# A two-layer hybrid block on one core: all input units of the second mixer in rounded halves

## The reference, cut to what matters

```
p = x @ w_in                               # 1024 x 6144: 24 units of 256 columns
p_rwkv, p_conf, p_short, p_gate = split(p) # 7, 2, 3 and 12 units
y_a = rwkv7(p_rwkv)   # a linear recurrence over time, 8 heads of 64; it normalizes the key kk by head
y_b = silu(layernorm(causal_conv31(u))) @ w_o, u = p_conf[:256] * sigmoid(p_conf[256:])
y_c = (gb * causal_conv3(gc * h)) @ w_o
g = sigmoid(p_gate)
x = layernorm(alpha * x + (g_a*y_a + g_b*y_b + g_c*y_c) @ w_out)
x = layernorm(alpha * x + feed_forward(x)) # dense in layer 0, 8 experts with top 2 in layer 1
```

## Time and profile before

| | |
|---|---|
| median of 3 runs | 2674.24 us (2672.26 to 2674.87) |
| the profiled execution | 2675.59 us, its span 2673.8 us |
| mean granted TensorE clock | 0.981 of full speed |
| TensorE busy | 2580.9 us, 97% of the span |
| VectorE busy | 1787.9 us, 67% |
| ScalarE busy | 1251.7 us, 47% |
| the two mixers | about 889 to 1223 us and 1414 to 1748 us |

### The profile page before, as it was taken

The page is one execution under the profiler, slowest core; times in us unless marked ns, Lnnn a source line. Parts: engine busy times, 40 slices in busy tenths (PEclk is TensorE's granted clock), DMA queues, the critical chain, the costliest instruction groups (busy, mean ns, idle before and its releaser), DMA issues.

```text
span 2673.8 us, 41063 instructions
## 1 busy us (share of the span) xinstructions
PE 2580.9 (97%) x16370; PEld 2186.1 (82%) x16370; DVE 1787.9 (67%) x2178; ACT 1251.7 (47%) x1443; POOL 116.3 (4%) x125
## 2 busy tenths in 40 slices
PE   7999999999999999999998999989999999999997
PEld 6886998878799988767998887678888888888886
DVE  5654776855577546345545553378988988988988
ACT  4442544542344331113334211057777777777775
POOL 1100000200000001200000111000000000000000
PEclk9999999999999999999999999989999999999999
DMA  6333543423455331135553321289999999998995
GB/s 250 111 142 142 184 183 128 152 95 128 181 183 187 141 126 65 64 126 197 189 186 130 110 80 64 79 317 349 351 358 341 349 355 346 346 357 346 347 360 204
DMA packets 77035, 558.16 MB, mean 209 GB/s; under 512 B 8673, under 2 KB 8801, under 8 KB 9569
## 3 DMA queue, kind: packets, MB, share of 16 engines
q1 hardware_dynamic: 76032, 550.93, 55.3%
q0 software_dynamic: 864, 5.24, 0.5%
HBM read 555.09 MB, written 1.05 MB: 208 GB/s over the span
## 4 chain that ended last, share of the span: by engine, by line
PE 60%; issue 35%; DVE 3%; ACT 2%; DMA 1%; POOL 0%; SPq 0%; POOLq 0%; DVEq 0%; ACTq 0%
PE bank L612 25%; PE bank L587 9%; PE bank L635 7%; PE bank L663 4%; PE bank L597 4%; PE bank L621 1%; DMA cst<-in_cst 1%; PE bank L896 1%; PE bank L881 1%; PE bank L893 1%; PE bank L739 1%; PE bank L723 1%; PE bank L731 1%; PE bank L722 1%; DVE ring_lo L1608 1%
## 5 line engine op out<-in xcount | busy, mean ns | idle before, releaser
L2162 DVE TENSOR_TENSOR w_lo<-ring,w_hi 128x2048 fp32r<-128x2048 f32 x216 | 486.3, 2289 | 53.9 <-ACT w_hi L1464 52.8
L1464 ACT ACTIVATE w_hi<-ring 128x2048 fp32r<-128x2048 f32 x216 | 405.1, 1917 | 20.5 <-PE bank L1060 16.9
L1060 PE MATMUL bank<-w_hi,xe_hi 128*128 128x512 f32 x792 | 311.2, 393 | 1.2
L1529 DVE TENSOR_TENSOR w_lo<-ring,w_hi 128x2048 fp32r<-128x2048 f32 x99 | 226.8, 2291 | 125.2 <-ACT w_hi L1159 122.9
L1060 PE MATMUL bank<-w_hi,xe_lo 128*128 128x512 f32 x792 | 308.5, 390 | 0.0
L1060 PE MATMUL bank<-w_lo,xe_hi 128*128 128x512 f32 x792 | 308.5, 390 | 0.0
L612 PE MATMUL bank<-x_hi,w_hi 128*128 128x256 f32 x1056 | 300.1, 284 | 0.8 <-DVE x_lo L1520 0.7
L612 PE MATMUL bank<-x_lo,w_hi 128*128 128x256 f32 x1056 | 299.6, 284 | 0.0
L612 PE MATMUL bank<-x_hi,w_lo 128*128 128x256 f32 x1056 | 299.5, 284 | 0.0
L1159 ACT ACTIVATE w_hi<-ring 128x2048 fp32r<-128x2048 f32 x99 | 189.5, 1914 | 219.3 <-DMA ring<-in_stream 113.8
L587 PE MATMUL bank<-xT,ring 128*128 128x256 f32 x1088 | 256.2, 388 | 1.1 <-ACT Z L1387 1.1
(11 more groups left out here) (340 smaller groups left out, 4868.5 us busy)
## 6 DMA issues: line engine op xcount, KB each, us to landing
ring<-in_stream SPq DMA_DIRECT2D x431, 1024.0 KB, 4.9
yT<-in_stream SPq DMA_DIRECT2D x54, 1024.0 KB, 6.4
xT<-in_stream SPq DMA_DIRECT2D x27, 1024.0 KB, 6.8
Z<-in_stream SPq DMA_DIRECT2D x8, 1024.0 KB, 7.8
norm_rows<-in_rows POOLq DMA_DIRECT2D x4, 1024.0 KB, 7.8
cst<-in_cst SPq DMA_DIRECT2D x1, 1889.0 KB, 20.6
par<-in_par SPq DMA_DIRECT2D x1, 1502.0 KB, 17.2
xres<-in_x SPq DMA_DIRECT2D x2, 512.0 KB, 7.0
```

The lines of the kernel that those rows point to most:

```text
L1060: r = mm(banks[4 + j % 2], a[:, k, :], moe_part(b, i)[:, q * 512:(q + 1) * 512], start=(k == 0 and a is xe_hi and b is w_hi), stop=(k == K ...
L1464: act_(moe_part(w_hi, at), moe_slot(at), ACT.Copy).then_inc(*A.done("moe_hi", at))
L1529: v.tensor_tensor(part(w_lo, n), slot(f0 + n), part(w_hi, n).bitcast(F32), ALU.subtract)\
L2162: v.tensor_tensor(moe_part(w_lo, at), moe_slot(at), moe_part(w_hi, at).bitcast(F32), ALU.subtract)\
```

## The change

Units 7 to 23 of the mixer are also multiplied as rounded halves: three fp32r matmuls for each product in place of one float32 product. Each of these 17 units gets a copy by ScalarE and a subtraction by VectorE. The high halves rotate over five buffers (`LATE_HI`) that lie in memory which is free at the time; `late_user(n)` is the unit that used the buffer before, and the copy waits until TensorE has finished it. ScalarE does the copy of unit n + 2 just before it evicts unit n, or just after where the buffer was unit n's own. The subtractions are put by hand into VectorE's list (`split(7)` to `split(23)`).

The float32 copies of the transposed x (`xT_out`) go; the halves of x move to `x1_hi` and `x2_lo`, the latter in the place of `norm_rows`. So GpSimd loads `norm_rows` for the first layer norm only when the last input unit is done, no longer at the kernel's start and after layer 0.

The fill of the start stage is 6, 18, 4 in place of 12, 12, 4: `kksum` comes six quarters earlier. Taps are spread otherwise: 4 ahead of the gram, 2 and then one at each step in the levels of p = 0, then 2, 2 and 4 in the two chunks of p = 0, 4 in level 0 of p = 1 and 2 in level 1. `short_conv` moves from the levels of p = 0 to the last level of p = 1. Some scratch buffers of the levels move in memory.

```diff
+        x2_lo = rounded("x2_lo", 0, KT * SEQ, norm_rows_at).rearrange("p (k n) -> p k n", k=KT)
         mix_hi = rounded("mix_hi", 6144, SPLIT * UNIT)
+        late_hi = [[rounded(f"late_hi{n}", at, UNIT, gates_at)] for n, at in enumerate((0, UNIT, 2 * UNIT))]
+        late_hi += [[rounded("late_hi3", 15872, UNIT)],
+                    [rounded("late_hi4", 15872 + UNIT, UNIT // 2), rounded("late_hi5", 0, UNIT // 2, yT_at)]]
...
-        START_FILL, GRAM_FILL, CHUNK_FILL = (12, 12, 4), 4, (1, 1, 1)
+        LATE_HI = {n: i for i, ns in enumerate(((9, 12), (8, 11, 14, 16), (7, 10, 13, 15, 17), (18, 20, 22), (19, 21, 23))) for n in ns}
...
+        def late_user(n):
...
+            return max((m for m in LATE_HI if m < n and LATE_HI[m] == LATE_HI.get(n)), default=None)
+
+        START_FILL, GRAM_FILL, CHUNK_FILL = (6, 18, 4), 4, (1, 1, 1)
...
+                    sp.wait_ge(*(T.of("sumsq", l, len(QK_PAIRS) - 1) if u < MIX2_0 else T.of("unit", (MIX2_0, MIX2_1)[l] + N_IN2 - 1)))
+                    if u >= MIX2_0:
+                        sp.wait_ge(*T.of("o", l, 3))
                 sp.dma_start(slot(u), stream[u]).then_inc(s_slot[HOME[u]], 16)
...
                 def quarter(n, q):
-                    u = u0 + n
+                    u, c = u0 + n, q // 2
                     if q == 0:
-                        pe.wait_ge(*loaded(u))
+                        pe.wait_ge(*V.of("lo", u))
                         pe.wait_ge(*(V.of("shift", l, n - 4) if n - 4 < 7 else A.of("in2", l, n - 4)))
-                    r = features(banks[4 + n % 4], slot(u), q // 2, range(4 * (q % 2), 4 * (q % 2) + 4))
+                    for k in range(4 * (q % 2), 4 * (q % 2) + 4):
+                        at = k * 256 + c * P
+                        hi = late_hi[LATE_HI[n]]
+                        whole = hi[0][:, at:at + P] if len(hi) == 1 else hi[k // 4][:, at % 1024:at % 1024 + P]
+                        for w, x in ((whole, x1_hi), (whole, x2_lo), (slot_lo(u)[:, at:at + P], x1_hi)):
+                            r = mm(banks[4 + n % 4][:, c * SEQ:(c + 1) * SEQ], w, x[:, k, :],
+                                   start=(k == 0 and w is whole and x is x1_hi), stop=(k == KT - 1 and w is not whole))
                     if q == 3:
                         r.then_inc(*T.done("unit", u))
                 for n in range(7):
                     pe.wait_ge(*V.of("lo", u0 + n))
-                    if n == 2:
-                        pe.wait_ge(*A.of("xT", "b2", l))
-                        pe.wait_ge(*V.of("xT", "b2", l))
                     if n >= 4:
                         pe.wait_ge(*V.of("shift", l, n - 4))
-                    features_split(banks[4 + n % 4], (part(mix_hi, n), slot_lo(u0 + n)), (x_hi, x_lo),
+                    features_split(banks[4 + n % 4], (part(mix_hi, n), slot_lo(u0 + n)), (x1_hi, x2_lo),
...
 
+                    if n >= N_IN2:
+                        return
                     sc.wait_ge(*loaded(u0 + n))
-                    if n >= SPLIT:
-                        sc.wait_ge(*T.of("unit", u0 + n - SPLIT))
-                    act_(part(mix_hi, n), slot(u0 + n), ACT.Copy).then_inc(*A.done("hi", u0 + n))
+                    if n < 7:
+                        if n >= SPLIT:
+                            sc.wait_ge(*T.of("unit", u0 + n - SPLIT))
+                        act_(part(mix_hi, n), slot(u0 + n), ACT.Copy).then_inc(*A.done("hi", u0 + n))
+                        return
+                    if late_user(n):
+                        sc.wait_ge(*T.of("unit", u0 + late_user(n)))
+                    if n == 18:
+                        sc.wait_ge(*V.of("ends", l))
+                    parts = late_hi[LATE_HI[n]]
+                    for i, to in enumerate(parts):
+                        w = UNIT // len(parts)
+                        act_(to, slot(u0 + n)[:, i * w:(i + 1) * w], ACT.Copy).then_inc(*A.done("hi", u0 + n))
                 if l == 0:
...
                     split(n)
-                x_hi_out("b2", l, None)
-                sc.wait_ge(*V.of("x_lo", "b2", l, KT - 1))
-                xT_out("b2", l, None)
+                x_hi_out("b2", l, None, x1_hi)
...
                 sc.wait_ge(*V.of("omu", l))
                 for n in range(7):
-                    if n + 2 < 7:
+                    split(n + 2)
+                    unit(n)
+
+                def unit_and_split(n):
+                    if late_user(n + 2) != n:
                         split(n + 2)
                     unit(n)
-                fill = Filler(lambda n, q: None, unit)
+                    if late_user(n + 2) == n:
+                        split(n + 2)
+                fill = Filler(lambda n, q: None, unit_and_split)
...
+                    parts = [part(mix_hi, n)] if n < 7 else late_hi[LATE_HI[n]]
+                    for i, hi in enumerate(parts):
+                        at = slice(i * (UNIT // len(parts)), (i + 1) * (UNIT // len(parts)))
+                        v.tensor_tensor(slot_lo(u)[:, at], slot(u)[:, at], hi.bitcast(F32), ALU.subtract).then_inc(*V.done("lo", u))
...
-                x_lo_out("b2", l, None)
-                xT_out("b2", l, None)
+                x_lo_out("b2", l, None, x1_hi, x2_lo)
...
+                split(7)
                 ve.wait_ge(*A.of("sig", l))
...
                         .then_inc(*V.done("cum", l))
+                split(8)
+                split(9)
                 for i in range(2):
                     ve.wait_ge(*T.of("kksum", l, 1))
                     v.tensor_scalar(flat(t3)[:, i * 512:(i + 1) * 512], banks[i], 1e-24, None, ALU.max)\
                         .then_inc(*V.done("kkms", l))
+                split(10)
                 ve.wait_ge(*A.of("kknorm", l))
                 v.reciprocal(flat(t3), flat(t3)).then_inc(*V.done("kkrn", l))
                 own()
                 v.tensor_tensor(flat(kk), flat(kk), flat(t3), ALU.mult).then_inc(*V.done("kk", l))
+                split(11)
...
+                split(12)
...
-                conf_some(8)
+                split(13)
+                conf_some(4)
+                split(14)
...
                     if p == 0:
-                        conf_some(6)
+                        split(15)
+                        conf_some(2)
+                    else:
+                        split(20)
...
                             if p == 0:
-                                conf_some(2 if lv < 3 else 1)
-                        if p == 0 and lv == 4:
-                            short_conv()
+                                conf_some(1)
+                            elif lv == 0:
+                                conf_some(2)
+                        if p == 0 and lv in (0, 2, 4):
+                            split(16 + lv // 2)
+                        if p == 1 and lv == 0:
+                            split(21)
                         if p == 1:
                             if lv == 0:
                                 group_norm_start(0)
                             if lv == 1:
                                 group_norm_end(0)
+                            if lv == 1:
+                                conf_some(99)
...
+                            if lv == 4:
+                                split(22)
+                                short_conv()
...
                         v.tensor_copy(us[ch, :], banks[1][ch, :]).then_inc(*V.done("us", l, c))
+                        if c == 1:
+                            conf_some(2)
                         ve.wait_ge(*T.of("s", l, c))
                         if c:
...
                         own()
+                        if c in (0, 2):
+                            split((19, 23)[p])
+                        if p == 0:
+                            conf_some((2, 4)[cc])
...
                 group_rstd(1)
+                po.wait_ge(*T.of("unit", u0 + N_IN2 - 1))
+                load_norm_rows(l, 0)
                 ln("ln1", l, "x1")
                 load_norm_rows(l, 1)
 
             g.memset(mh, -0.5).then_inc(*G.done("minus_half"))
-            g.dma_start(norm_rows, rows_d[0, 0:2 * D].partition_broadcast(P)).then_inc(s_norm_rows, 16)
...
             if n_stages == 4:
-                load_norm_rows(1, 0)
                 mixer(1, MIX2_1)
```

More of the change, by code:

```diff
@@ L228, in emit @@
         norm_rows = sb("norm_rows", 2 * D)
+        norm_rows_at = nc.sbuf_base - 4 * 2 * D
         group_rows = sb("group_rows", 2 * 512)
@@ L235, in emit @@
         yT = sb("yT", KT * SEQ)
+        yT_at = nc.sbuf_base - 4 * KT * SEQ
         small = sb("small", 512)
@@ L460, in emit @@
         gram = Z[:, 12288:14336].rearrange("p (h n) -> p h n", h=8)
-        invs = [x.rearrange("p (h n) -> p h n", h=8) for x in (Z[:, 16384:16896], v_.rearrange("p t n -> p (t n)")[:, 512:1024])]
-        lev = Z[:, 16896:17408].rearrange("p (h n) -> p h n", h=8)
+        invs = [x.rearrange("p (h n) -> p h n", h=8) for x in (Z[:, 14336:14848], v_.rearrange("p t n -> p (t n)")[:, 512:1024])]
```

(21 more changed lines are left out.)

## The result

The changed kernel takes 2682.61 us (median of 17 runs, 2676.61 to 2686.71) against 2673.57 for the kernel before in the same job: ratio 1.0033, 95% interval 1.0026 to 1.0040, so 9 us slower. I had forecast 2671.2. The time lies just outside my range (2658 to 2681), next to the rival with the falling clock (2680.6). That this number came so near is partly luck: the waits came out shorter than its sum had them, and the clock cost more. Its profiled execution took 2682.99, with a span of 2681.2.

The account below looks back on a forecast made before the run. TensorE, busy in 97% of the span, was taken as the bound. Per mixer, 21.4 us saved less 19.0 of waits and 2.1 of clock left 0.3, 0.6 for both; with 2.4 for norm rows, 2671.2 us, range 2658 to 2681.

Parts of the forecast that it names:

- the rival with the falling clock: Clock falls in new waits of start stage and levels of p = 1: 6.8 us a mixer, 2680.6 us; chance 0.18.
- Clock: Lower clock behind the new waits of 4.4 and 3.0 us: 2.1 us lost a mixer, bounds 0 and 6.8.
- the sign of being wrong: Low halves coming in time, or windows at 0.50 clock standing in number after the new waits.
- What the change saves: Fill in both mixers: 1.26 us less a unit in one piece, 0.31 a lone quarter; 21.4 us a mixer.
- Start stage: TensorE waits for VectorE's low halves of units 10 to 12: 2.4, 4.4 and 0.3 us, sum 7.1 a mixer.
- The prediction's sentence on 12 quarters: Start stage: behind 12 quarters unit 10 would come right after `kksum` and wait all of 10.9 us.
- Gram of p = 0: Unit 15's subtraction blocks GpSimd's chain for 2.0 us, and 1.26 saved is given back: wait 3.3 us.
- Gram of p = 1: Taps delay the gram's eviction, so `m` waits 2.5 us, 1.8 more; GpSimd's blocked chain adds a wait of 2.0.
- Levels of p = 1: Taps and unit 21's subtraction make VectorE late: waits of 3.0 and 1.0 us, 0.4 for later squares, sum 4.4.
- Levels and chunks of p = 0: Taps and subtractions fit; one wait of 0.4 us where ScalarE copies unit 17 ahead of evicting `lev`.
- VectorE late into the last chunks: Rival: late from levels of p = 1, VectorE delays units 22 and 23 by 1 to 2 us each: 2677; chance 0.08.
- Norm rows: Kernel's start: without their 1 MB load the constants land earlier, 2.4 us gained, bounds 0 and 2.5.

Follow-up runs that it names:

- The idle matmuls: The changed kernel with matmuls that nothing reads put into TensorE's new waits: 2672.34 us, ratio 0.9998 to the kernel before.
- the run with two moves: The changed kernel with unit 10's halves made ahead of `kkms` and the taps moved away from the gram and level 1 of p = 1: 2651.61 us, ratio 0.9918.
- the run with the power moved: The changed kernel with the group norm's power behind level 2's masks of p = 1 in GpSimd's list: 2676.71 us, ratio 1.0018.
- the kernel before with idle matmuls: The kernel before with five float32 matmuls that nothing reads in the wait ahead of each mixer's small-rank stage: 2668.07 us, ratio 0.9979.

## Why the prediction was wrong

**Clock: the step that failed.** I booked 2.1 us a mixer, with bounds 0 and 6.8. By half of the new time at the lower level it was 10.4 and 11.8 (6.8 for the second against the other execution of its old code), and filling the waits gave 9 us back in both mixers together. Windows at the lower level stood behind the new waits in number, which I had named as the sign of being wrong. Two things were wrong in the term. I took only the waits of 4.4 and 3.0 as able to bring the clock down, since one of 3.1 at 1678 had not the earlier trace rows. But the waits of 2.79 and of 2.69 us brought 3.4 us at the lower level each, by the windows above, and the two of 2.39 and 2.48, ten microseconds apart, 6.7. And one wait after which the clock stayed up was no bound. The wait of 1678 is that for the last activations ahead of `project_out`; in the first mixer of the same execution it is 3.09 long, and behind it stands

```profile
1156.00:1164.00 8.00, 7.22 (x26) 6.07 (x27) 3.56 (x6) 0.73 (x2) 0.00 (x0) 0.79 0.85 360
```

that is 3.4 us at the lower level. By my own price, 3.4 us of time for a fall, the upper bound had to be that for each of the five new waits over 2 us, 17 a mixer; half of it already makes the forecast a slower kernel. The idle matmuls showed by experiment that these waits bring the clock down, and that it costs 9 us in all.

**What the change saves.** As priced: a unit in one piece behind the gram takes 5.92 us, its ends included, and from the first matmul of a lone quarter to the next instruction it is 1.61 (1007.24 to 1008.85 in the run with two moves).

**Start stage.** Unit 10 waited 2.39 (I had 2.4) and unit 11 2.48 (4.4). In the run with the power moved, where unit 10 kept its clock, the second is 4.0: the slow clock stretched unit 10 to 7.45 us and so ate part of the wait. Wait and clock are not independent terms; where one is there the other is partly paid. The prediction's sentence on 12 quarters was wrong: I had moved `kksum` in my mind and left ScalarE's list as it was.

**Gram of p = 0.** Predicted 3.3 with 2.0 of blocking, measured 2.79 with 2.78 - 0.90 = 1.9. When GpSimd's instruction started at 1002.60, 2.19 of the subtraction was left, and moving the subtraction away brought 0.91 back. By the Trainium skill (SBUF — State Buffer, section "SBUF: two separate sides") the loser is shut out for the whole instruction. The trace agrees to within 0.3 us, as to what is left of the subtraction.

**Gram of p = 1.** `m` waited 2.69 (2.5). GpSimd's chain was blocked as foreseen, but the fill ahead of it ran at the lower clock and hid half: 0.96 in place of 2.0. In the second mixer, where this fill ran at 1.00, it is 2.18.

**Levels of p = 1.** I had 3.0 for VectorE, and it was 4.57 for GpSimd. I left out that GpSimd's list has the group norm's power, which waits for VectorE's variance, ahead of level 2's masks. Those 1.2 beyond VectorE's own 3.4 are what the move of the power showed.

**Levels and chunks of p = 0**, and VectorE late into the last chunks: a wait for ScalarE in the levels (L900) has 0.2 in all that the kernel before had not, where I took 0.4, and no new wait stands in the chunks.

**Norm rows.** 2.4 booked, 1.3 shown. The constants landed at 23.62, near the 23 that I had foretold, but that is no proof: in the kernel before with idle matmuls, which keeps the load, they landed at 23.25. The first mixer of the profiled execution starts 2.9 earlier, but one code's start alone differs by more than that from one execution to another, as said.

So the waits came to 15 to 16 where I had 19, the norm rows to 1 less than booked, and the clock, priced at half, to 8 to 10 more a mixer (5 in the second against the other execution). Since a slow clock and the waits trade, these are not separate causes: with both waits and clock as booked the mixers would have cost 21.1, and they cost 25.6 and 28.1. Left open is what decides whether one wait brings the clock down or not. In the second mixer of the changed kernel `m` waits the same 2.69, up to 1602.30, and the clock stays up; it is down behind the wait of 2.18 that follows, up to 1611.06:

```profile
1603.00:1611.00 8.00, 5.88 (x48) 5.67 (x48) 3.64 (x4) 2.09 (x3) 7.08 (x8) 1.00 0.12 26
1611.00:1619.00 8.00, 7.94 (x120) 7.50 (x120) 2.30 (x6) 1.17 (x3) 2.06 (x3) 0.79 0.26 110
```

That an execution's second mixer can hold 6.8 us at the lower level and another's 16.7, with the same code there, was seen and not explained.

## What to carry to other kernels

Price each new wait of TensorE twice: its length, and half of what it then runs at the lower clock. Here that is some 2 us more for each wait over 2; where the work behind it waits for another engine anyway, part comes back, and filling the waits gave some 1 us for each. Two engines' in-order lists decide a wait together: before an operation is put in, ask of each list what else is queued behind it (the reciprocal, the masks, the gram's eviction), and put it where that engine idles for another. When a change saves work and the time doesn't move, keep the engine busy in its waits with work that nothing reads; that shows how much of the loss is the clock.

## What the runs showed of the hardware

- In the first mixer waits of 2.69 and 2.79 us brought the granted clock from 1.00 to a mean of 0.79 over the 8 us around or behind them; with matmuls in them it stayed at 1.00. It isn't so each time: in the second mixer of the same execution the clock stayed at 1.00 over the 8 us behind a wait of 2.69.
- 20 rounded matmuls of 128x256, or five float32 ones, in a wait of 3.0 us keep the clock up in the 16 us around it (1.00 for 0.79). They ended before what TensorE waited for: 0.6 and 0.8 us of the wait were left.
- A slower clock and the wait behind it trade: the wait for unit 11 is 2.48 us where unit 10 ran partly at the lower level (7.45 us), and 4.0 where unit 10 took 5.92.
- VectorE and GpSimd hold each other up both ways, one after the other. GpSimd's L2322 (2.35 us in the kernel before, where it is L2268) starts just behind a subtraction, takes 4.37 and ends at 946.61. The next subtraction starts before that and takes 3.76 in place of 2.29, so it ends 2.15 behind GpSimd's:

```profile
942.08 2.27 DVE L1837 TENSOR_TENSOR ring_lo<-ring,late_hi 128x2048 fp32r<-128x2048 f32 x1
942.24 4.37 POOL L2322 TENSOR_TENSOR Z<-Z 128x1024 f32<-128x1024 f32 x1 [247.72 <-DVE Z L1857]
...
945.00 3.76 DVE L1837 TENSOR_TENSOR ring_lo<-ring,late_hi 128x2048 fp32r<-128x2048 f32 x1 [0.66 <-ACT late_hi L1337]
```
